# Gate and up matrices of the experts requested in halves of their columns

## The reference, cut to what matters

```python
for layer in range(2):
    h = h + mixer(rms_norm(h, mix_norm), w_in, w_out)
    h = h + hier_moe(rms_norm(h, ffn_norm), w_group, b_group, w_fine, b_fine, w_gate, w_up, w_down)
out = rms_norm(h, final_norm)

# hier_moe: each token picks one of 4 groups and 2 of its 8 experts, and for each expert e
hid = silu(xb @ w_gate[e]) * (xb @ w_up[e])      # 1024 -> 512, twice
y   = hid @ w_down[e]                            # 512 -> 1024
```

## Time and profile before

| what | value |
|---|---|
| median of 3 executions | 1177.79 us (1173.85 to 1178.16) |
| the profiled execution | 1177.3 us |
| its span, first to last instruction | 1175.2 us |
| TensorE busy | 870.3 us, 74% of the span |
| VectorE, ScalarE, GpSimd busy | 370.6, 226.8, 35.7 us |
| data moved | 441.20 MB, mean 375 GB/s |
| mean granted TensorE clock | 0.872 |

### The profile page before, as it was taken

One profiled execution on the slowest core, in us unless ns is written; L12 is line 12 of the kernel. 1 busy time (PEld: TensorE's weight loads), 2 busy tenths in 40 slices (PEclk: granted clock), 3 DMA queues, 4 the chain that ended last, 5 costly groups with the idle time before them and its releaser, 6 DMA issues.

```text
span 1175.2 us, 21530 instructions
## 1 busy us (share of the span) xinstructions
PE 870.3 (74%) x9064; PEld 539.3 (46%) x9064; DVE 370.6 (32%) x942; ACT 226.8 (19%) x594; POOL 35.7 (3%) x51
## 2 busy tenths in 40 slices
PE   7998979957575757574799999797666666566655
PEld 5875446534242424242378755464343434343422
DVE  4875343312121212121268525232121212121212
ACT  4554101100000000000155651011000000000002
POOL 1002000000000000000010120000000000000000
PEclk8999999988787988887889999898787879887877
DMA  9957579999999999999994575799999999999994
GB/s 348 310 219 301 209 298 424 428 429 428 429 429 428 428 429 429 429 428 428 409 368 189 225 304 216 323 424 428 428 428 428 428 429 428 428 429 428 428 426 170
DMA packets 51261, 441.20 MB, mean 375 GB/s; under 512 B 8848, under 2 KB 9360, under 8 KB 26640
## 3 DMA queue, kind: packets, MB, share of 16 engines
q1 hardware_dynamic: 51072, 440.06, 90.3%
q10 hardware_dynamic: 144, 0.52, 0.1%
HBM read 439.53 MB, written 1.05 MB: 375 GB/s over the span
## 4 chain that ended last, share of the span: by engine, by line
DMA 39%; PE 39%; SPq 8%; another core or an unknown queue 5%; DVE 5%; ACT 3%; issue 1%; POOL 0%; POOLq 0%; ACTq 0%; DVEq 0%
DMA ring<-in_w_expert_up 38%; PE bank L905 12%; PE bank L968 4%; PE bank L924 4%; SPq L405 3%; SPq L401 3%; PE bank L813 3%; PE bank L815 3%; PE bank L814 3%; PE bank L937 2%; PE bank L887 2%; SPq L402 1%; DMA cst<-shape_consts 1%; DVE split L1137 1%
## 5 line engine op out<-in xcount | busy, mean ns | idle before, releaser
L905 PE MATMUL bank<-ring,scratch 128*32 128x256 f32 x4096 | 310.0, 469 | 256.0 <-DMA ring<-in_w_expert_up 254.6
L905 PEld LDWEIGHTS bank<-ring,scratch 128*32 128x32 f32 x4096 | 160.5, 135 | 403.0 <-issue 273.0
L1334 DVE TENSOR_SCALAR scratch<-scratch 128x128 f32<-128x128 f32 x64 | 14.5, 227 | 633.7 <-ACT scratch L639 611.8
L638 ACT ACTIVATE scratch<-bank 128x128 f32<-128x128 f32 x64 | 17.8, 278 | 572.1 <-PE bank L905 553.4
L924 PE MATMUL bank<-ring,h 128*32 128x256 f32 x2048 | 127.2, 390 | 0.0
L813 PE MATMUL bank<-split,h_high 128*128 128x512 f32 x192 | 79.3, 413 | 8.0 <-DVE split L1137 6.4
L924 PEld LDWEIGHTS bank<-ring,h 128*32 128x32 f32 x2048 | 60.9, 111 | 45.8 <-issue 13.8
L1137 DVE SCALAR_TENSOR_TENSOR split<-ring,gains,split 128x512 fp32r<-128x512 f32 x96 | 68.3, 749 | 38.9 <-ACT split L683 35.2
L937 PE MATMUL bank<-h 32*128 32x256 f32 x1024 | 73.3, 400 | 4.7 <-ACT h L646 4.7
L815 PE MATMUL bank<-split,h_high 128*128 128x512 f32 x192 | 76.7, 400 | 0.0
L814 PE MATMUL bank<-split,h_low 128*128 128x512 f32 x192 | 76.6, 399 | 0.0
(11 more groups left out here) (151 smaller groups left out, 644.6 us busy)
## 6 DMA issues: line engine op xcount, KB each, us to landing
ring<-in_w_expert_gate SPq DMA_DIRECT2D x64, 2048.0 KB, 47.6
ring<-in_w_expert_up SPq DMA_DIRECT2D x64, 2048.0 KB, 49.2
ring<-in_w_expert_down SPq DMA_DIRECT2D x64, 2048.0 KB, 48.9
ring<-in_w_in_even SPq DMA_DIRECT2D x5, 2048.0 KB, 17.9
ring<-in_w_in_odd SPq DMA_DIRECT2D x5, 2048.0 KB, 22.3
ring<-in_w_out_even SPq DMA_DIRECT2D x2, 2048.0 KB, 8.4
ring<-in_w_out_odd SPq DMA_DIRECT2D x2, 2048.0 KB, 11.2
ring<-in_w_in_even SPq DMA_DIRECT2D x2, 1024.0 KB, 8.4
```

The costliest lines, as they stand in the source:

```text
L905: last = pe.matmul(psum[6][32 * j:32 * j + 32, 0:2 * P].rearrange("p (a s) -> p a s", a=2), xT[:, c, SLOTS * k:SLOTS * k + SLOTS], ring[:, ...
```

## The change

A pair is asked for in four requests in place of two: the first half of the gate's columns, the first half of the up's, then the second halves. Each half has a semaphore of its own, `pair_arrived[l][k][0]` and `[1]`. The gate/up product waits for the first half ahead of chunk 0 and for the second ahead of chunk 4. Seven sets of semaphores that were one per layer become one for both layers, with thresholds that go on counting; that keeps the number of semaphores about as it was.

```diff
-        pair_arrived = [sems(f"pair_arrived{l}_", GE) for l in range(LAYERS)]
+        pair_arrived = [[sems(f"pair_arrived{l}_{k}_", 2) for k in range(GE)] for l in range(LAYERS)]
...
-        k_cleared = sems("k_cleared", LAYERS)
+        k_cleared = sem("k_cleared")
...
             def load_pair(l, row, k):
                 unit = PAIR_AT[k]
-                sp.dma_start(ring[:, unit, :], gate_rows[row]).then_inc(pair_arrived[l][k], 16)
-                sp.dma_start(ring[:, unit + 1, :], up_rows[row]).then_inc(pair_arrived[l][k], 16)
+                for half, arrived in enumerate(pair_arrived[l][k]):
+                    cols = slice(half * (UNIT // 2), half * (UNIT // 2) + UNIT // 2)
+                    sp.dma_start(ring[:, unit, cols], gate_rows[row][:, cols]).then_inc(arrived, 16)
+                    sp.dma_start(ring[:, unit + 1, cols], up_rows[row][:, cols]).then_inc(arrived, 16)
...
-                pe.wait_ge(pair_arrived[l][k], (group_no(r, g) + 1) * 32)
                 if k == 0:
                     pe.wait_ge(xT_ready[l], group_no(r, g) * 2 + 1)
                 for c in range(C):
+                    if c % (C // 2) == 0:
+                        pe.wait_ge(pair_arrived[l][k][c // (C // 2)], (group_no(r, g) + 1) * 32)
                     if k == 0 and c == C // 2:
                         pe.wait_ge(xT_ready[l], group_no(r, g) * 2 + 2)
...
-                pe.wait_ge(assigned[l], 1)
+                pe.wait_ge(assigned, T * l + 1)
```

More of the change, by code:

```diff
@@ L348, in build @@
         dve_attn = sems("dve_attn", LAYERS)
[L350 to L355, removed]
+        logits_done = sem("logits_done")
+        gmax_ready = sem("gmax_ready")
+        gexp_done = sem("gexp_done")
+        assigned = sem("assigned")
+        counts_done = sem("counts_done")
+        pos_done = sem("pos_done")
         first_gates = sem("first_gates")
@@ L559, in _ @@
                 some = n_items[l] // 2
[L560 to L563, removed]
+                pool.memset(pairs[HEAD:P, 0:some, 0, :], 0.0).then_inc(k_cleared, 1)
+                pool.wait_ge(k_cleared, 2 * l + 1)
+                pool.memset(pairs[0:HEAD, 0:some, 1, :], 0.0).then_inc(k_cleared, 1)
+                pool.wait_ge(k_cleared, 2 * (l + 1))
                 for m in range(HEADS[l]):
@@ L607, in copy_qkT @@
                     if t == 0:
-                        act.wait_ge(k_cleared[l], 2)
+                        act.wait_ge(k_cleared, 2 * (l + 1))
                     kv = kT.rearrange("p (a b) s -> p a b s", b=2)
@@ L747, in _ @@
                 for t in range(T):
-                    act.wait_ge(gmax_ready[l], t + 1)
+                    act.wait_ge(gmax_ready, T * l + t + 1)
                     act.activation(expg[:, t, :], lg[:, t, 0:GROUPS], ACT.Exp, bias=gv[:, t:t + 1],
                                    accum_out=gv[:, 2 + t:3 + t])
-                    act.activation(gv[:, 4 + t:5 + t], gv[:, 6 + t:7 + t], ACT.Exp).then_inc(gexp_done[l], 1)
+                    act.activation(gv[:, 4 + t:5 + t], gv[:, 6 + t:7 + t], ACT.Exp).then_inc(gexp_done, 1)
                 act.wait_ge(gate_steps[l], GATE_STEPS)
@@ L1002, in logits @@
                                      w_rt[:, l, c, :], start=(c == 0), stop=(c == C - 1))
-                last.then_inc(logits_done[l], 1)
+                last.then_inc(logits_done, 1)
             pe.wait_ge(warm_ready, 1)
@@ L1066, in _ @@
                 keep_warm(2, cst[:, 0:512])
-                pe.wait_ge(assigned[l], 2)
-                pe.matmul(psum[4][:, 0:32], ones, asg[:, 1, :], start=False, stop=True).then_inc(counts_done[l], 1)
-                pe.matmul(psum[6][:, 32:64], before, asg[:, 1, :], start=False, stop=True).then_inc(pos_done[l], 1)
+                pe.wait_ge(assigned, T * l + 2)
+                pe.matmul(psum[4][:, 0:32], ones, asg[:, 1, :], start=False, stop=True).then_inc(counts_done, 1)
+                pe.matmul(psum[6][:, 32:64], before, asg[:, 1, :], start=False, stop=True).then_inc(pos_done, 1)
                 keep_warm(1, cst[:, 0:512])
@@ L1251, in route @@
             def route(l, t, link):
-                dve.wait_ge(logits_done[l], t + 1)
+                dve.wait_ge(logits_done, T * l + t + 1)
                 bank, bias = psum[4 + t], b_rt[:, l, :]
@@ L1272, in route @@
                 dve.tensor_tensor(gv[:, 6 + t:7 + t], best[:, 1:2], best[:, 0:1], ALU.subtract)\
-                   .then_inc(gmax_ready[l], 1)
+                   .then_inc(gmax_ready, 1)
                 link(dve.max_index(idx_u[:, T + t, :], best, masked[:, t, :]))
@@ L1280, in route @@
                 dve.tensor_tensor(asg[:, t, :], chosen[:, t, 0, :], chosen[:, t, 1, :], ALU.add)\
-                   .then_inc(assigned[l], 1)
+                   .then_inc(assigned, 1)
             def places(l, link):
-                dve.wait_ge(gexp_done[l], T)
+                dve.wait_ge(gexp_done, T * (l + 1))
                 by = gv[:, 8:10]
@@ L1289, in places @@
                 dve.reciprocal(by, by).then_inc(first_gates, 1)
-                dve.wait_ge(counts_done[l], 1)
+                dve.wait_ge(counts_done, l + 1)
                 link(dve.reduce_max(cnt[:, 0:1], psum[4][:, 0:32], AX.X))
@@ L1295, in places @@
                 dve.tensor_copy(rounds_i[:, l:l + 1], cnt[:, 1:2]).then_inc(rounds_ready[l], 1)
-                dve.wait_ge(pos_done[l], 1)
+                dve.wait_ge(pos_done, l + 1)
                 link(dve.scalar_tensor_tensor(out=posm[:, :, 0:EXPERTS],
```

## The result

| | before | changed |
|---|---|---|
| median | 1177.18 us (15 runs) | 1180.74 us (15 runs) |
| lowest to highest | 1173.46 to 1179.11 | 1178.45 to 1183.91 |
| span of the profiled execution | 1175.2 us | 1178.1 us |

The ratio is 1.0032, 95% interval 1.0021 to 1.0043: 3.8 us slower, a small loss that 15 runs can tell from zero. It is under the half per cent named as "no change" above.

The account below looks back on a forecast made before the run. The prediction took the expert stages as bound by transfers and the rest by computation. A toll of 8.3 us less a gain of 5.5 us gave + 2.8 us on 1177.3, 1180.1 us, range 1172 to 1187.

Parts of the forecast that it names:

- The bound: Expert stages are bound by transfers at 428 GB/s; TensorE's 335 us of waits at the gate/up product are no prize.
- Part 2, the toll: Full stream of both layers: 8 KB rows add 16 packets per pair and engine at 9.3 ns, costing 8.3 us.
- rival (b): Full stream of both layers: packets cost 13.7 ns, completions count, second halves run at 1.2 GHz: + 9.8 us; chance 0.16.
- The doubt about the 2 KB rows' strided source: QKV weights of layer 1: 2 KB rows may be slow because cut from 12 KB source rows; toll's lower bound nothing.
- The three cycles per packet: Inside the DMA engine: fixed overhead of 3.5 ns per packet, making the toll 3.2 us and the whole change − 2.3 us.
- rival (a): Expert transfers: packets almost free, toll nothing to half of 8.3 us, total 1171.8 to 1175.9 us; chance 0.25.
- Part 1, the gain: Last gate/up product of each layer: only half stands behind the last landing, saving 5.5 us together, bounds 4.0 and 7.0.
- half a product is 3.3 us at the low level: Last gate/up products: 32 matmuls at 1.2 GHz take 3.3 us, priced at 0.102 us each.
- the middle between the clock's levels: Last gate/up products: gain taken between low and high clock, 2.4 us in layer 1 and 3.1 in layer 0.
- Next in line: Layer ends: layer 1's last down matrix and first weight block each have 3.7 us of slack and don't become late.
- The queue's depth: DMA queue: if depth counts rows, 48 us in flight fall to 29, above SyncE's longest wait of 17.7; no dry queue.
- Sum: Whole kernel: + 8.3 − 5.5 = + 2.8 us on the profiled execution's 1177.3, giving 1180.1 us.

Follow-up runs that it names:

- 4 KB rows: Kernel before the change, with every pair's gate and up matrices each in four requests of 4 KB rows and one wait ahead of the product: 1203.62 us, ratio 1.0230.
- the toll alone: Changed kernel with both halves waited for ahead of chunk 0, same requests but no early start: 1185.4 us, ratio 1.0087 to before.
- the halves experiment: Changed kernel with whole requests for all pairs but each layer's last, which comes in halves on its own semaphores: 1173.65 us, ratio 0.9971 to before.
- the quarters: Kernel of the halves experiment with each layer's last pair in quarters of its columns, four waits two chunks apart: 1171.89 us, ratio 0.9958 to before.

## Why the prediction was right, point by point

- **The bound.** Right. The idle time of the product's matmuls behind the up matrix fell from 254.6 to 218.2 us over the whole span, and the kernel was not faster for it; the stages went with the rate of the transfers.
- **Part 2, the toll.** Right, in mechanism and size: 9.3 ns per added packet and 8.3 us were forecast, 424 to 425 GB/s. Measured are 424 GB/s, 8.2 us by the landings (7.6 to 9.1 over the three kernels with such pieces), 9.3 to 10.2 us by the timed runs without the early start, 10.1 ns per packet from the 4 KB rows. Taking the two throughputs (428 and 387 GB/s) and not the packets' own durations (13.7 ns) was the better choice; the 13.7 of rival (b) is outside the interval of the 4 KB run. The doubt about the 2 KB rows' strided source was not needed: 16, 8, 4 and 2 KB rows lie near one line (428, 424, 415 and 387 GB/s, the middle two with a third of the bytes still in 16 KB rows).
- **The three cycles per packet.** The Trainium skill, "DMA: Bandwidth & Descriptors", section "Why small descriptors are slow (HBM only)", gives them, 3.5 ns as an estimate from the page. The 4 KB run has 9.1 to 11.0 ns per added packet, so for these rows neither that estimate nor rival (a) holds as the whole cost.
- **Part 1, the gain.** The mechanism is right: half the product stands behind the landing. The term of 5.5 us was sized too high: 3.4 us against the trace of before, below the lower bound of 4.0, and 4.7 against the trace of the toll alone. The step that failed is "half a product is 3.3 us at the low level". It came from 25 matmuls counted in a window of 2.6 us; that window and the next count 70 in a product of 64, so most of those at the edge between them are counted twice and the price per matmul comes out too low. A product wholly at full clock takes 3.66 us, so half of one at half the clock takes 3.66 too, and 3.64 was measured. Taking the middle between the clock's levels was wrong here as well: in the changed kernel all four halves of the two last products ran at 0.50. Why they did, when the halves experiment had three of four at full clock, stays open. The timed runs give 3.4 us for the gain alone (1.8 to 4.9), which leaves 5.5 out, and 6.5 for the difference to the toll alone, which lets it in; the two are not the same quantity, since the halves ran at other clocks.
- **Next in line.** The last down matrix, with 3.7 us of slack, was not reached by the halves and was by the quarters. "It holds", said of layer 1's first weight block, came true in the changed kernel with 0.8 us left and failed in the two kernels that split the last pair alone in halves. There it was the last to arrive and cost some 0.9 us. The prediction's own upper gain of 3.8 us for layer 0 was more than the slack of 3.7, so it could not have been had in full.
- **The queue's depth.** Forecast 29 us in flight if it counts rows; measured 31, and no hole.
- **Sum.** + 2.8 forecast, + 3.8 measured (2.5 to 5.1). The toll came out as said, the gain 2.1 us smaller by the traces of before and after. That the sum is only 1.0 off is partly luck: by toll and gain of the two traces it would be + 4.8.

## What to carry to other kernels

In a stage bound by transfers, starting the consumer earlier pays once, behind the last transfer, while anything that makes the packets smaller is paid on every one of them. Split the last load alone: here that turned + 0.3% into − 0.3 to − 0.4%. Then look at what arrives next: a slack of 3.7 us was used up by the halves in one layer and by the quarters in the other. Price a smaller row from two stretches of the same trace with known row sizes and full queues, by their throughput.

## What the runs showed of the hardware

- A stream with its gate and up matrices in requests of 64 neighbouring partitions moved 247 GB/s, the same for 64 alternate partitions 428, with all 16 engines reported busy in both. "DMA busy" doesn't say that the engines are quick.
- How far the queue runs ahead shrinks with the packets, and a little with the requests: a request landed 48 us behind its issue with 16 KB rows, 42 to 44 with twice the requests at the same rows, 35 to 37 with 8 KB pieces in as many requests, 31 with both, 18 to 21 with 4 KB rows. In none of them did the queue run dry.
- Into the full queue, requests of 128 rows took the same time to issue whatever their bytes: 4.23 us for the 2 MB up matrix of the earlier trace rows, 4.23 to 4.24 us for 1 MB in the halves experiment and 4.24 to 4.25 us for 512 KB in the quarters (both in layer 0, behind a backlog of 2 MB matrices). With the issues of the last pair in halves, layer 1's first weight block was asked for 8.7 us later than before (543.14 against 534.44).
- A pause of 2.9 us on TensorE was followed by full clock once (1.93 us for 32 matmuls, granted clock 1.00) and by the low one once (3.21 us, 0.59) in the same execution.
